# A hybrid decoder trunk in split fp32: the two passes that split each weight chunk are made in halves

## What is computed

```python
def swiglu_ffn(h, w_in, w_out):
    gate, up = jnp.split(h @ w_in, 2, axis=-1)
    return (jax.nn.silu(gate) * up) @ w_out

for i in range(DEPTH):
    mods = jnp.split(c_act @ ada_w[i] + ada_b[i], N_MOD, axis=-1)
    sh1, sc1, g1, sh2, sc2, g2, sh3, sc3, g3 = mods
    h = modulate(rms_norm(x, norm_g[i, 0]), sh1, sc1)
    x = x + 0.5 * g1[:, None, :] * swiglu_ffn(h, ffn_w_in[i, 0], ffn_w_out[i, 0])
    h = modulate(rms_norm(x, norm_g[i, 1]), sh2, sc2)
    m = retention(h, ...) if i % 2 == 0 else s5_layer(h, ...)
    x = x + g2[:, None, :] * m
    h = modulate(rms_norm(x, norm_g[i, 2]), sh3, sc3)
    x = x + 0.5 * g3[:, None, :] * swiglu_ffn(h, ffn_w_in[i, 1], ffn_w_out[i, 1])
return rms_norm(x, final_g)
```

## Time and profile before

| | |
|---|---|
| median of 3 runs | 2340.04 us (2337.68 to 2340.14) |
| profiled execution, time and span | 2335.91 us, 2334.1 us |
| PE busy | 2184.4 us, 94% of the span |
| DVE busy | 1179.2 us, 51% |
| ACT busy | 598.5 us, 26% |
| mean granted TensorE clock | 0.954 of full |
| DMA | 313.10 MB, 134 GB/s |

### The profile page before, as it was taken

How to read it: one execution, slowest core, us unless ns; L and a number is a source line. 1 busy time by engine, 2 the same in 40 slices (tenths; PEclk the granted TensorE clock), 3 DMA queues, 4 the chain that set the end, 5 groups by cost and what they waited for, 6 DMA issues and landing times.

```text
span 2334.1 us, 26357 instructions
## 1 busy us (share of the span) xinstructions
PE 2184.4 (94%) x10312; PEld 1814.4 (78%) x10312; DVE 1179.2 (51%) x1493; ACT 598.5 (26%) x485; POOL 39.4 (2%) x43
## 2 busy tenths in 40 slices
PE   6899999889999998999999799999979889999995
PEld 5787888778888886888877677778858777888884
DVE  6667544555355334555576666643447544333231
ACT  2222222222132132222211222332131224343212
POOL 2000000000000000000000000000000000000000
PEclk9999999989999998999999899999986898999997
DMA  6455535332222141655536334443667222232320
GB/s 238 144 183 177 193 127 167 130 112 95 72 94 94 54 144 58 212 168 191 162 118 207 130 122 143 140 139 122 230 194 260 77 91 72 97 101 90 99 81 36
DMA packets 261228, 313.10 MB, mean 134 GB/s; under 512 B 31520, under 2 KB 218144, under 8 KB 258864
## 3 DMA queue, kind: packets, MB, share of 16 engines
q1 hardware_dynamic: 220128, 278.47, 36.1%
q10 hardware_dynamic: 41040, 33.82, 4.6%
HBM read 288.93 MB, written 27.53 MB: 136 GB/s over the span
## 4 chain that ended last, share of the span: by engine, by line
PE 51%; issue 35%; DVE 6%; DMA 3%; ACT 2%; POOL 1%; SPq 1%; DVEq 0%; POOLq 0%; ACTq 0%
PE ps L1409 15%; PE ps L1411 15%; PE ps L1410 15%; DMA w_raw<-in_ffn_w_out 1%; ACT w_hi L470 1%; DMA dt<-in_s_log_dt 1%; DVE w_lo L752 1%; PE ps L1559 1%; DVE tabs L989 1%; DMA w_raw<-in_ffn_w_in 1%; DVE ada_acc L763 1%; PE ps L1662 1%; PE ps L1664 1%; PE ps L1649 1%; POOL dt L456 0%
## 5 line engine op out<-in xcount | busy, mean ns | idle before, releaser
L1409 PE MATMUL ps<-h_hi,w_lo 128*128 128x512 f32 x1792 | 716.5, 400 | 25.0 <-DVE w_lo L752 14.0
L1411 PE MATMUL ps<-h_hi,w_hi 128*128 128x512 f32 x1792 | 707.6, 395 | 0.0
L1410 PE MATMUL ps<-h_lo,w_hi 128*128 128x512 f32 x1792 | 707.6, 395 | 0.0
L752 DVE TENSOR_TENSOR w_lo<-w_raw,w_hi 128x2048 fp32r<-128x2048 f32 x174 | 390.2, 2242 | 459.8 <-ACT w_hi L470 458.9
L470 ACT ACTIVATE w_hi<-w_raw 128x2048 fp32r<-128x2048 f32 (+1 forms) x176 | 329.1, 1870 | 495.4 <-PE ps L1411 154.8
L1409 PEld LDWEIGHTS ps<-h_hi,w_lo 128*128 128x128 f32 x1792 | 343.8, 192 | 97.7 <-issue 15.4
L1411 PEld LDWEIGHTS ps<-h_hi,w_hi 128*128 128x128 f32 x1792 | 342.6, 191 | 73.6
L1410 PEld LDWEIGHTS ps<-h_lo,w_hi 128*128 128x128 f32 x1792 | 344.0, 192 | 69.7
L1409 PE MATMUL ps<-g_hi,w_lo 128*128 128x512 f32 x832 | 330.4, 397 | 6.6 <-DVE w_lo L752 6.6
L1411 PE MATMUL ps<-g_hi,w_hi 128*128 128x512 f32 x832 | 329.3, 396 | 0.0
L1410 PE MATMUL ps<-g_lo,w_hi 128*128 128x512 f32 x832 | 329.2, 396 | 0.0
(11 more groups left out here) (203 smaller groups left out, 1580.9 us busy)
## 6 DMA issues: line engine op xcount, KB each, us to landing
w_raw<-in_ffn_w_in SPq DMA_DIRECT2D x87, 1024.0 KB, 6.8
ada_raw<-in_ada_w SPq DMA_DIRECT2D x128, 512.0 KB, 5.3
w_raw<-in_ffn_w_out SPq DMA_DIRECT2D x32, 1024.0 KB, 6.9
w_raw<-in_ret_w_in SPq DMA_DIRECT2D x24, 1024.0 KB, 5.3
w_raw<-in_ffn_w_out SPq DMA_DIRECT2D x16, 768.0 KB, 4.7
tb<-s_rec SPq DMA_DIRECT2D x6, 2048.0 KB, 8.5
w_raw<-in_ret_w_out SPq DMA_DIRECT2D x8, 1024.0 KB, 4.9
w_raw<-in_s_w_glu SPq DMA_DIRECT2D x8, 1024.0 KB, 5.8
```

What stands on the lines that cost most here:

```text
L752: V.tensor_tensor(w_lo[k % 2][:, 0:r, :], w_raw[k % 2][:, 0:r, :], raw_f32(w_hi[k % 2][:, 0:r, :]), ALU.subtract).then_inc(w_lo_done, 1)
L1409: nc.tensor.matmul(o, wl, xh, start=start, stop=False)
L1410: nc.tensor.matmul(o, wh, xl, start=False, stop=False)
L1411: return nc.tensor.matmul(o, wh, xh, start=False, stop=stop)
```

## The change

Both passes of a split are issued as two instructions, tiles 0 to 3 and tiles 4 to the last (`HALF` is 4). Two semaphores are added: ACT's first half raises `w_hi_half`, DVE's first half waits for that and raises `w_lo_half`. The second halves use `w_hi_done` and `w_lo_done` as the whole passes did. `chunk` waits for `w_lo_half` ahead of its first tile and for `w_lo_done` ahead of its fifth. SP, `values` and `gate_tile` wait for `w_lo_done`, as before; `begin` and `split_first` are left as they were, and the new semaphores start at 3 to stand for the two chunks that `begin` splits.

```diff
@@ ACT: split_hi
                 act.wait_ge(w_landed[k % 2], landed(n, k))
                 act.wait_ge(w_used, n)
-                copy(w_hi[k % 2][:, 0:r, :], w_raw[k % 2][:, 0:r, :]).then_inc(w_hi_done, 1)
+                copy(w_hi[k % 2][:, 0:HALF, :], w_raw[k % 2][:, 0:HALF, :]).then_inc(w_hi_half, 1)
+                copy(w_hi[k % 2][:, HALF:r, :], w_raw[k % 2][:, HALF:r, :]).then_inc(w_hi_done, 1)
...
+            act.sem_inc(w_hi_half, 3)
@@ DVE: split_lo
+                dve.wait_ge(w_hi_half, n + 2)
+                V.tensor_tensor(w_lo[k % 2][:, 0:HALF, :], w_raw[k % 2][:, 0:HALF, :],
+                                raw_f32(w_hi[k % 2][:, 0:HALF, :]), ALU.subtract).then_inc(w_lo_half, 1)
                 dve.wait_ge(w_hi_done, n + 2)
-                V.tensor_tensor(w_lo[k % 2][:, 0:r, :], w_raw[k % 2][:, 0:r, :],
-                                raw_f32(w_hi[k % 2][:, 0:r, :]), ALU.subtract).then_inc(w_lo_done, 1)
+                V.tensor_tensor(w_lo[k % 2][:, HALF:r, :], w_raw[k % 2][:, HALF:r, :],
+                                raw_f32(w_hi[k % 2][:, HALF:r, :]), ALU.subtract).then_inc(w_lo_done, 1)
...
+            dve.sem_inc(w_lo_half, 3)
@@ PE: chunk
-                pe.wait_ge(w_lo_done, n + 2)
+                pe.wait_ge(w_lo_half, n + 2)
                 s = k % 2
                 for t in range(r):
+                    if t == HALF:
+                        pe.wait_ge(w_lo_done, n + 2)
...
+HALF = KT // 2
```

More of the change, by code:

```diff
@@ L209, in build @@
         w_hi_done, w_lo_done, w_used = sem("w_hi_done"), sem("w_lo_done"), sem("w_used")
+        w_hi_half, w_lo_half = sem("w_hi_half"), sem("w_lo_half")
         consts, par_in, x_in = sem("consts"), sem("par_in"), [sem(f"x_in{t}") for t in range(OUT_PAIRS)]
```

## The result

The changed kernel takes 2318.61 us (median of 4 runs, 2316.62 to 2320.12), the kernel before 2339.14 us on the same chip (median of 4, 2337.68 to 2340.14). The ratio is 0.9912 with a 95% interval of [0.9895, 0.9929]: 20.5 us faster. The forecast was 2321.4 us in a range of 2315 to 2332. The profiled execution of the changed kernel took 2316.62 us, its span is 2314.8 us, and it ran at a mean granted clock of 0.958 (before: 2335.91, 2334.1, 0.954).

What follows compares the result with a forecast made beforehand. PE, busy 94% of the span, bounds the kernel; only its 27.1 us of waits for `w_lo` offer gain. Stalls and chain 15.3 plus clock 2.5 and 0.8 make 18.6 us: 2340.0 - 18.6 = 2321.4 us, range 2315 to 2332.

Steps and rivals of the forecast that it cites:

- Latency of a split: From ACT's start, first half ready for PE after 2.38 us instead of 4.29, whole split after 3.47 instead of 4.24.
- Chunks 2, 10, 16, 68, 92, 98, 136: PE's stalls: gains 1.9, 1.8, 1.0, 2.25 at 2, 10, 16, 68; about 0 left at 92, 98; 1.9 at 136.
- chunks 14 and 16: FFN 0: PE, early after chunk 10, would wait again here for 0.2 to 0.4 us.
- Chunk 2: FFN 0: gain 1.9 of the 3.80 us stall, and 1.65 us of half clock behind it avoided.
- Chunk 36: Retention's first `values`, still waiting for the whole split: gain 0.6 of 6.50 us.
- FFN 1: 2.25 us at its input's stall, 5.6 in the output chain, 0.8 from the clock; norm starts 13 to 16 us sooner.
- Chunk 94: FFN 1's output phase: PE's stall of 3.22 us becomes about 1.4, with full clock behind it.
- The clock: Stalls at chunks 2, 10, 94, shortened below 2.09 us, leave full clock: 2.5 us in FFN 0, 0.8 in FFN 1's output.
- Rival 1: The clock falls behind the shortened stalls as before, so only 15.3 us are gained: 2324.7 us; chance 0.25.
- Rival 2: Halves' fixed costs come through in FFN 0, FFN 1's output and FFN 2, taking 7 to 14 us: 2332; chance 0.13.
- Rival 3: PE's wait ahead of tile 4 holds back the weight load, 156 times 0.188 us: slower, 2350.7 us; chance 0.05.
- Rival 4: The change does nothing; PE's start is set by something other than the first half, say the DMA; chance 0.03.

Runs made afterwards that it cites:

- experiment 2: The kernel before, whole passes kept, with only a second, satisfied PE wait for `w_lo_done` ahead of tile 4 of every chunk; 2342.37 us, ratio 1.0005.
- experiment 5: Halves only in FFN 2 and FFN 3 (chunks 101 to 134 and 142 to 175), whole passes elsewhere, against the kernel before; 2343.5 us, ratio 1.0009.
- experiment 6: Halves only in FFN 1 (chunks 66 to 100), whole passes elsewhere, against the kernel before; 2332.8 us, ratio 0.9957.

## Why the prediction was right, point by point

- **Latency of a split.** 2.38 us to the first half and 3.47 us to the whole were forecast, 2.37 and 3.45 measured. Both came from durations of the same operation and width on other tiles and from the spacing of starts, not from half of a whole pass.
- **Chunks 2, 10, 16, 68, 92, 98, 136.** The stalls after are 1.74, 1.47, 0.36, 0, 0, 0 and 2.05 us in the first profile, within 0.2 us of the forecast. The small waits forecast for chunks 14 and 16 are there too (0.46 and 0.36). Their premise is not: PE was to be 6.9 us early after chunk 10, and it starts chunk 11 only 3.4 us early in the first pair of profiles (192.61 to 189.23) and 5.3 us in the mean of three.
- **Chunk 2: a term that brought next to nothing.** Its stall is 2.06 us shorter, but PE starts chunk 3 at 96.90 where it had been 96.81; in the mean of three profiles each it is 0.5 us sooner, where the forecast had 1.9 for the stall and 1.65 for the clock. Two things took the gain. The chunk landed later: ACT starts its split at 80.64, 81.69 and 81.07, and at 79.84, 79.87 and 80.50 with whole passes. No edit of the change stands ahead of that load, and why it is later stays open. And PE runs at half clock behind the stall for 6.2, 5.4 and 5.0 us, and for 3.5, 4.4 and 6.0 before.
- **Chunk 36.** From the start of `g_lo` to the end of the split it is 481.45 + 1.22 - 479.17 = 3.50 us, and was 4.09: 0.59 sooner, forecast 0.6. The stall itself repeats too badly to show it (6.50, 5.50 and 5.59 us with whole passes, 5.39, 5.91 and 5.61 in the changed kernel). The stage as a whole shows no gain (-0.65 us), which the spread of profiles covers.
- **FFN 1.** 8.65 us were forecast from chunk 66 to 100 (2.25 + 5.6 + 0.8). The mean of the profiles is 3.85 + 4.98 = 8.83 us, and halves in this stage alone bring 9.0. POOL's `rstd` behind FFN 1 starts 13.1 us sooner in the first pair of profiles and 14.0 in the mean, where 13 to 16 were forecast. How the 8.83 are made up differs from the forecast, as said below.
- **Chunk 94.** The stall is 2.22, 2.58 and 2.57 us, forecast 1.4. The forecast started from 3.22, and the other two profiles with whole passes have 2.63 and 2.19. The load is no clear cause: from its issue on SP to ACT's start it is 1228.05 - 1221.28 = 6.77 us in the changed kernel's first profile and 6.30 in that of before, but over three profiles each it is 6.77, 7.51 and 6.99 against 6.30, 7.25 and 6.81. The rows are SP's issue and ACT's start in the changed kernel's first profile:

```profile
1221.28 10.75 SPq L271 DMA_DIRECT2D w_raw<-in_ffn_w_out  x3
```

```profile
1228.05 2.00 ACT L471 ACTIVATE w_hi<-w_raw 128x1024 fp32r<-128x1024 f32 x2 [18.56 <-DMA w_raw<-in_ffn_w_out]
```

  That a load might land later once it starts sooner was named as what could make the forecast wrong. At chunk 94 the spread hides it, and it wasn't tried.
- **The clock, 3.3 of the 18.6 us: the step that failed.** It said that a stall shorter than the 2.09 us of chunk 68 leaves the clock alone. At chunk 10 it does, in 7 of 7 profiles, and the clock falls there in all 7 with stalls from 2.50 us. At chunk 2 the forecast put down to the stall of 3.80 us a half clock that was there before it began: in the trace of before PE stood 5.16 us for `ada` until 78.46, the clock fell at 77.4, and the stall of chunk 2 began at 80.33. Shortening that stall could not keep the clock up. That the wait for `ada` brings the fall fits in time, in all 14 profiles; no run took that wait away. The row is PE's in the changed kernel:

```profile
79.40 1.87 PE L1440 MATMUL ps<-ones,ada_acc 128*128 128x1 f32 x8 [5.06 <-DVEq L780]
```

  At chunk 94 it held in one of three profiles of the changed kernel. The Trainium skill ("TensorE: Matmul & The Clock Gate", Part 1) says that the window in which the chip looks runs freely against the program. By that rule the same stall can meet a fall in one execution and not in the next, and the three profiles at chunks 94 and 136 agree.
- **A term that was missing: POOL's `rstd` behind FFN 2, 1.07 us.** The forecast asked what the longer busy time of DVE would cost and not who waits beside a long instruction of DVE. The rows were there: 3.80 us of wait at this norm, of 10.5 us in six. The Trainium skill ("SBUF — State Buffer", "SBUF: two separate sides") says that DVE and GpSimd share a pair of ports under an exclusive lock held for a whole instruction, by a DVE operation with two inputs in SBUF against a GpSimd operation that reads it. The trace agrees: `rstd` ends 0.86 us behind the end of DVE's instruction in both kernels. It differs in one thing: by the page the one that starts first has the ports, and here POOL's shown start is 0.37 us ahead of DVE's and POOL is the one that waits. POOL's wait in the list of the kernel before:

```profile
PE ps L1445 <- POOL rstd L430: 10.5, 6, 3.8
```

- **Why the total was near all the same: in part luck.** The forecast was 15.3 us of stalls and chain and 3.3 of clock; the profiles have some 12.3 (11.4 + 0.9) and 5.9. The clock was to come back at chunks 2, 10 and 94. The runs give it at chunk 10 always, at 94 and 136 at times, at 2 never, and at 68 and 92, where the forecast had none, in two of three profiles. `rstd`'s 1.07 us and 1.6 us more than forecast in the input part of FFN 1 stand against what chunk 2 lacks. In FFN 1's input part the forecast took chunk 68's stall as 2.09 us with the full clock behind it, as in its one profile. The other two profiles with whole passes have 2.86 and 2.38 us there, and both run at half clock behind it (0.51 over 3.4 us in experiment 2, and this in the second profile of the kernel before):

```profile
948.80:952.00 3.20, 3.20 (x9) 2.55 (x8) 1.55 (x3) 2.82 (x2) 0.00 (x0) 0.50 0.00 0
```

  Of the 0.41 us in FFN 3 it is known that they lie in chunk 142, not what brings them.
- **The rivals.** Rival 1 (2324.7 us, no gain from the clock) is right about the outcome at chunk 2 and in two of three profiles at 94, and wrong at chunk 10; its time is 6 us above the median. Rival 2 (fixed costs come through, 2332) falls with experiment 5 in FFN 2 and FFN 3 and with experiment 6 in FFN 1; FFN 0 wasn't tried alone. The fixed costs themselves are there: 2 x 1.05 - 1.909 = 0.19 us on ACT and 2 x 1.22 - 2.292 = 0.15 us on DVE. Because a second half starts before the first one's shown end, ACT's busy time grew by 16.0 us only (forecast up to 36) and DVE's by 7.6 (forecast 14 to 28). Rival 3 (2350.7) falls with experiment 2. Rival 4 falls with 2.37 us in place of 4.29.

## What to carry to other kernels

Before a chain of producers ahead of the bounding engine is cut in two, count only the stalls at which the chain starts late, price the halves from rows of the same operation at the new width, and check that the consumer's work on the first part is longer than the producers' on the second: a cut at 4 or 2 of 8 gave the same time, a cut at 1 of 8 took 6 us more (2327.92 against 2321.95 us for the changed kernel on the same chip), with new waits at the second tile. Much of such a gain can come from the overlap of the producers alone (11 of some 20 us here), so that is worth doing even where the consumer can't take a half. Then ask who waits beside a long instruction of a shared engine, and look at the stall that is left: moving one split ahead of work that wasn't urgent brought another 5 us here.

## What the runs showed of the hardware that was not expected

- A stall of 1.61 us at chunk 94 was followed by 6.4 us at a granted clock of 0.51, and one of 2.88 us at chunk 136 by 3.9 us at 1.00. The length of a stall alone doesn't tell the clock behind it; at one place it can be either level in two executions of one kernel (chunk 94: 1.00 over 5.6 us, 0.50 over 5.6 and 6.0 us). And half clock behind a stall need not come from it: at chunk 2 the clock was at 0.50 before the stall began.
- A 128x4 operation on POOL takes 1.01 us alone, 1.60, 1.86 or 2.40 us beside two DVE passes of which the first is 0.36, 0.63 or 1.16 us, and 3.46 us beside a single one of 2.23 us: each time it ends 0.86 us behind the end of the first.
- 156 more waits in PE's queue, all satisfied, changed the time by a ratio of 1.0005 [0.9995, 1.0015], with the matmuls 0.24 and 0.23 us apart across the wait.
- Two halves in a row on ACT take 2.00 us in place of 1.909, not 2.10: an instruction starts before the shown end of the one ahead.
